# Weights of a two-block transformer kernel in units of 512 columns instead of 1024, with the same bytes of buffer

## The reference

```python
# first block, twice
h = h + _mixer(rmsnorm(h), w_in, w_ret_o, w_sb_o, w_out)   # retention, stick-breaking attention, gates
h = h + (silu(g) * u) @ w_down                             # g, u = rmsnorm(h) @ w_gate_up, FF = 2816
...
# second block, for layer in range(2)
x = x + 0.5 * swiglu(rms_norm(x, g[0]), ffn1_w_in[layer], ffn1_w_out[layer])
x = x + mixed            # layer 0: forgetting and differential attention; layer 1: convolution and banded attention
x = x + memory_cross_attention(rms_norm(x, g[2]), rms_norm(mem, g[3]), ...)
x = x + 0.5 * swiglu(rms_norm(x, g[4]), ffn2_w_in[layer], ffn2_w_out[layer])
```

## Time and profile before

| what | us |
|---|---|
| median of three runs | 1864.65 |
| the profiled execution's own time | 1865.1 |
| its span, first to last instruction | 1862.7 |
| TensorE (PE) busy in the span | 1857.9 |
| VectorE (DVE) busy | 1310.3 |
| ScalarE (ACT) busy | 1119.3 |
| GpSimd (POOL) busy | 369.0 |

### The profile page before, as it was taken

The page is one execution under the profiler, slowest core; times in us unless marked ns, Lnnn a source line. Parts: engine busy times, 40 slices in busy tenths (PEclk is TensorE's granted clock), DMA queues, the critical chain, the costliest instruction groups (busy, mean ns, idle before and its releaser), DMA issues.

```text
span 1862.7 us, 25413 instructions
## 1 busy us (share of the span) xinstructions
PE 1857.9 (100%) x9293; PEld 1623.7 (87%) x9293; DVE 1310.3 (70%) x1949; ACT 1119.3 (60%) x1678; POOL 369.0 (20%) x606
## 2 busy tenths in 40 slices
PE   9999999999999999999999999999999999999999
PEld 8888988888889888888888889888888888899888
DVE  6776776667777776666577886776666578977664
ACT  6776655557766655555468785654555467765553
POOL 2101233111001431122103001531122111102320
PEclk9999999999999999999999999999999999999999
DMA  9767789878578997798765567997798788758984
GB/s 316 236 186 229 222 258 299 260 233 253 166 221 242 292 287 232 219 272 255 238 180 191 174 191 204 281 274 237 225 255 252 227 265 242 216 157 232 255 258 138
DMA packets 289803, 436.43 MB, mean 234 GB/s; under 512 B 25548, under 2 KB 170416, under 8 KB 289424
## 3 DMA queue, kind: packets, MB, share of 16 engines
q1 hardware_dynamic: 260384, 352.41, 61.9%
q0 software_dynamic: 28832, 82.07, 16.3%
q10 hardware_dynamic: 464, 0.34, 0.1%
HBM read 396.43 MB, written 38.29 MB: 233 GB/s over the span
## 4 chain that ended last, share of the span: by engine, by line
PE 99%; DMA 0%; DVE 0%; SPq 0%; ACT 0%; issue 0%; ACTq 0%
PE M L1081 31%; PE M L1083 31%; PE M L1082 31%; PE AUX L1124 1%; PE AUX L1138 0%; PE AUX L1252 0%; DMA RAW<-in_w_in 0%; PE AUX L1244 0%; PE AUX L1242 0%; PE AUX L1279 0%; PE AUX L1167 0%; PE AUX L1295 0%; PE AUX L1323 0%; PE AUX L1296 0%; PE AUX L1297 0%; PE AUX L1324 0%
## 5 line engine op out<-in xcount | busy, mean ns | idle before, releaser
L1647 DVE TENSOR_TENSOR WL<-RAW,WH 128x1024 fp32r<-128x1024 f32 (+1 forms) x669 | 810.8, 1217 | 383.5 <-ACT WH L1358 380.9
L1358 ACT ACTIVATE WH<-RAW 128x1024 fp32r<-128x1024 f32 (+1 forms) x670 | 705.0, 1055 | 518.8 <-PE M L1083 469.7
L1081 PE MATMUL M<-WH,Bh 128*128 128x512 f32 (+1 forms) x1820 | 691.3, 380 | 0.6 <-ACT TMP L1401 0.3
L1082 PE MATMUL M<-WL,Bh 128*128 128x512 f32 (+1 forms) x1820 | 683.1, 375 | 0.0
L1083 PE MATMUL M<-WH,Bl 128*128 128x512 f32 (+1 forms) x1820 | 683.1, 375 | 0.0
L1081 PEld LDWEIGHTS M<-WH,Bh 128*128 128x128 f32 x1820 | 344.2, 189 | 50.6 <-issue 4.2
L1083 PEld LDWEIGHTS M<-WH,Bl 128*128 128x128 f32 x1820 | 344.2, 189 | 47.1
L1082 PEld LDWEIGHTS M<-WL,Bh 128*128 128x128 f32 x1820 | 344.4, 189 | 44.7
L1396 ACT ACTIVATE AS<-M,KEEP 128x256 f32<-128x256 f32 x132 | 55.3, 470 | 80.3 <-PE M L1083 78.7
L1081 PE MATMUL M<-WH,MTh 128*128 128x512 f32 x128 | 51.0, 398 | 0.0
L1082 PE MATMUL M<-WL,MTh 128*128 128x512 f32 x128 | 48.5, 379 | 0.0
(11 more groups left out here) (534 smaller groups left out, 2886.9 us busy)
## 6 DMA issues: line engine op xcount, KB each, us to landing
RAW<-in_ffn_w_in SPq DMA_DIRECT2D x352, 256.0 KB, 4.2
RAW<-in_w_in SPq DMA_DIRECT2D x103, 512.0 KB, 4.8
RAW<-in_w_gate_up SPq DMA_DIRECT2D x176, 256.0 KB, 4.4
RAW<-in_ffn_w_out SPq DMA_DIRECT2D x88, 512.0 KB, 4.6
RAW<-in_w_down SPq DMA_DIRECT2D x44, 512.0 KB, 4.9
RAW<-in_x_w_kv SPq DMA_DIRECT2D x32, 512.0 KB, 4.6
RAW<-in_even_w_in SPq DMA_DIRECT2D x24, 512.0 KB, 4.5
RAW<-in_odd_w_in SPq DMA_DIRECT2D x24, 512.0 KB, 5.4
```

The source lines that it names most:

```text
L1081: e.matmul(out, s.hi, wh, start=s.at0, stop=False)
L1082: e.matmul(out, s.hi, wl, start=False, stop=False)
L1358: e.activation(hi, raw, ACT.Copy).then_inc(k.w_hi, 1)
L1647: e.tensor_tensor(lo, raw, hi.bitcast(F32), ALU.subtract).then_inc(k.w_lo, 1)
```

## The change

It halves the unit and doubles the count of slots and buffers. The bytes of RAW (4 x 1024 = 8 x 512 columns), of WH and of WL (5 x 1024 = 10 x 512) stay. Nothing of `PLACES` and `LATER` changes. The first eight k-blocks were units of 1, 1, 2, 2 and 2 k-blocks and become eight units of one.

```diff
-UC = 1024
-NRAW = 4
-NHL = 5
+UC = 512
+NRAW = 8
+NHL = 10
...
-    first = [(0, 1), (1, 1), (2, 2), (4, 2), (6, 2)]
+    first = [(i, 1) for i in range(8)]
...
-            e.wait_ge(*((k.w_used, s.c.done - 3) if t else (k.tile_done, 1)))
+            e.wait_ge(*((k.w_used, s.c.done - 6) if t else (k.tile_done, 1)))
...
-                        p.add("nfld", p.now + 40.0).done = p.n_unit + 18
+                        p.add("nfld", p.now + 40.0).done = p.n_unit + 36
```

## The result

The changed kernel takes 1874.86 us (median of six runs, 1874.08 to 1875.79) against 1864.62 us for the kernel before (median of six, 1864.44 to 1866.2). The ratio is 1.0052, 95% interval 1.0043 to 1.0062. It is slower by 10.2 us, outside of the range of the prediction. The profiled execution took 1874.99 us, its span is 1872.9 us and the granted clock 1.0.

The account below looks back on a forecast made before the run. TensorE was taken as the bound, busy 1857.9 of 1862.7 us. Opening -0.6 and attention stages +1.4 gave +0.8 on the profiled 1865.1 us, so 1865.9, or 1865.5 against the median; range 1863.2 to 1871.

Parts of the forecast that it names:

- Attention stages: Attention stages: moved convs make some late steps miss their slack, +1.4 us, bounds 0 and 13.
- 21 close points: Attention stages: 21 releases of TensorE with under 0.45 us to spare; each can win 0.5 us or lose 0.6.
- Buffers that come free by halves: Weight buffers: release after each k-block raises the weights' lead from 6.9 to about 10 us, worth nothing where nothing waits.
- VectorE as the bound: Attention stages: added VectorE work overfills its busiest windows, costing 6 to 12 us, 1871 to 1877; chance 0.15.
- 135 and 94: Splits in halves: us of added busy time on ScalarE and VectorE, hidden behind TensorE in feed-forward stages at no cost.
- TensorE's waits and counts: TensorE's matmuls: 667 more waits and 667 more counts, taken as zero; upper bound 47 us, 17 us by the skill.
- The opening: First k-blocks: TensorE's stalls at 14.16 and 17.21 us shrink, a gain of 0.6 us, bounds 0 and 3.3.
- DMA: Weight loads: 934 DMAs become 1337, 575 us of queue issue time, taken as zero; bound 169 us inside queue waits.

Follow-up runs that it names:

- c_pairs: Changed kernel with convs placed two at a time at even k-blocks from unit 10 on; 1864.67 us, ratio 0.9995 to the kernel before.
- l_even_look9: Changed kernel with convs in pairs at even k-blocks and placed for 9 units ahead in place of 10; 1864.65 us, ratio 0.9998 to the kernel before.
- h_dve_halves: Kernel before with only VectorE's 1024-wide subtraction done as two 512-wide instructions; 1866.8 us, ratio 1.0008.
- m_handoff: Kernel before with both engines' splits done as two instructions and VectorE released after ScalarE's first half; 1866.23 us, ratio 1.0008.
- d_dma256: Kernel before with every weight DMA cut to 256 KB; 1865.29 us, ratio 0.9999.
- b_look9: Changed kernel with convs placed for 9 units ahead in place of 10, with ten buffers still; 1869.0 us, ratio 1.0020 to the kernel before.
- k_odd_look9: Changed kernel with convs in pairs at odd k-blocks and placed for 9 units ahead; 1878.0 us, ratio 1.0070 to the kernel before.
- f_pairs_look8: Changed kernel with convs in pairs at even k-blocks and placed for 8 units ahead; 1865.43 us, ratio 1.0007 to the kernel before, single runs 1864.51 to 1871.42.
- o_raw6: Changed kernel with six slots of RAW in place of eight; 1888.73 us, ratio 1.0125 to the kernel before.

## Why the prediction was wrong

**The step that failed is "Attention stages".** It took +1.4 us, one close point in three losing 0.2 us, within bounds of 0 and 13. Measured are 22 places with 11.0 us, 0.5 us each. The stages and the kind of step were the right ones; the size was too small by a factor of eight. It was taken near the low end, with the reason that the queues wait for TensorE for hundreds of us. That reason doesn't hold: a queue that waits for TensorE is not a queue with time to spare if the waiting instruction is a conv and a step that TensorE needs stands behind it. The section priced what a conv *lasts* (0.6 us), not what it *waits* (2.00 and 2.46 us in the two patterns above).

Its list of 21 close points missed many of the places as well. In 17 of the 22 the trace names the step for which TensorE waited. Before the change six of these 17 had ended more than 0.45 us ahead of TensorE's load, up to 1.67 us (L1961 at 1040 us) and with the longest stall's among them (0.51 us); they hold 3.5 us of the loss. Seven places lost more than the 0.6 us which was taken as the most that a point can lose, up to 1.69. So 21 is near 22, and the bound of 13 us held, partly by luck.

The waits of ScalarE's convs for TensorE were 392 before and are 673 after:

```profile
ACT WH L1358 <- PE M L1083: 447.7, 673, 3.0
```

The total of them fell (469.7 us before), while their number rose by 281. Each is a place at which a late step can be caught, if one stands behind it; c_pairs has 546 of them and loses nothing in sum. The step "Buffers that come free by halves", which called the longer lead "worth nothing where nothing waits", has the same fault: it looked at the lead of the weights, and never at who stands behind a conv.

**How the 10.2 us divide.** Taking the convs from the odd k-blocks removes all of it (c_pairs). One buffer in hand removes 5.9 us (1874.86 - 1869.0), by the wait for the buffer; the other 4.3 (1869.0 - 1864.65, to l_even_look9) go by the order alone, and where they were followed, by VectorE's wait for a copy. The split isn't a sum of two independent causes: with the convs at even places the buffer in hand brings nothing (1864.67 without it, 1864.65 with it). It also shortens the lead of the weights by a k-block: in l_even_look9's profiled execution (1866.54 us) the weights ran out twice, at 677 and 681 us, which cost some 2 us. The cause is the odd place, and the buffer wait is how more than half of it acts.

**VectorE as the bound, the rival with 0.15.** Its band, 1871 to 1877 us, holds the result. Its mechanism isn't what happened. It needs seven more k-blocks of work in a window that is full; VectorE's windows fell from 18.71 to 18.26 and from 19.47 to 17.18 us, and c_pairs and l_even_look9 do the same number of instructions at the time of before. That an occupation of 1 or 2 us exists isn't excluded (1.4 us in h_dve_halves, 1.2 in m_handoff, both at the edge of what can be told). That the result lies in its band is luck.

**What was right.** A 512-wide copy took 0.629 us and a subtraction 0.685, as taken. The groups rose by 820.7 - 703.5 = 117 us and 885.4 - 809.4 = 76 us, 135 and 94 being forecast; many halves run back to back and overlap. The feed-forward stages hid them: TensorE is busy for 20.00 us in the first window. The lead of the weights rose from 6.8 to 9.5 us in these stages and from 7.8 to 10.0 over all units after 20 us (medians), a rise from 6.9 to 10 being forecast. Its minimum fell, though, from 3.25 to 0.82 us.

*TensorE's waits and counts*: the starts in the feed-forward stage are still 0.216 us apart.

```profile
1322.24 0.38 PE L1081 MATMUL M<-WH,LA0h 128*128 128x512 f32 x1
1322.46 0.38 PE L1082 MATMUL M<-WL,LA0h 128*128 128x512 f32 x1
...
1323.54 0.38 PE L1081 MATMUL M<-WH,LA0h 128*128 128x512 f32 x1
```

From one k-block to the next it is 1.30 us, with a wait and a count in each now. l_even_look9 has all 667 more counts and stands at 0.9998. The Trainium skill ("TensorE: Matmul & The Clock Gate", The cost: per-tile semaphore tail) has some 26 ns for each increment, by which an estimate is 17 us for them. These runs don't show it, where one matmul in six counts.

*The opening*: both stalls are gone, 14.16 and 17.21 us in the earlier trace rows are now

```profile
14.05 0.38 PE L1081 MATMUL M<-WH,Bh 128*128 128x512 f32 x1
...
16.64 0.38 PE L1081 MATMUL M<-WH,Bh 128*128 128x512 f32 x1
```

The gain by 17 us is 0.57 us, for 0.6 forecast. It isn't the two stalls alone: TensorE also waits 0.8 us for the norm's gains ahead of 5.67 us (L1150) in this execution, and starts a little closer on either side of it make most of that good. *DMA*: nothing that d_dma256 shows. The prediction's 575 us of issues is a slip, 1337 x 0.42 is 562; nothing hangs on it.

**The numbers.** With 21 points under 0.45 us, and an upper bound of 13 us worked out for them, 0.15 for a loss of several us was too little, and 1871 as the upper end left out half of that bound.

**What stays open.** Of the 4.3 us of order, 1.6 lie between 1040 and 1042 us and 1.7 at 1586 us (before's time); the latter was followed through the queues, of the former only VectorE's wait ahead of L1865 was read. In b_look9 the stalls at 228 and 1699 us grew by 0.25 us each, and why is open. k_odd_look9's profiled execution is 1.5 us below its median, so its waits are those of one of its better runs. No version beats the kernel before by more than the measurement tells: the best are c_pairs with 0.9995 (0.9986 to 1.0004) and l_even_look9 with 0.9998. Places in `PLACES` set anew for convs at every k-block weren't tried.

## What to carry to other kernels

Where queues are in order and planned, halving a unit doubles the places at which an instruction asks for a buffer: ask of each what stands behind it, and whether the engine that frees the buffer needs that. The same holds for an instruction that waits for another engine's copy. Let a producer ask for a buffer one unit after it comes free, and keep the places when the grain changes (two halves where one whole stood); here the first was worth 5.9 us and the second all 10.2. Price such a place by the longest wait of the instruction in front (2 to 2.5 us here) less the slack of the step behind it, and not by the time that the instruction takes or by the average idleness of the engines.

## What the runs showed of the hardware

**A stall of 4 us costs more than itself.** In f_pairs_look8's longest run ScalarE waited for a small exchange through DRAM, with convs behind it:

```profile
677.38 0.63 ACT L1450 ACTIVATE FA1h<-HB1t 128x512 fp32r<-128x512 f32 x1 [7.08 <-DMA HB1t<-squares]
```

The lead was used up, TensorE waited 4.02 us, and then the granted clock was about half (windows of 5 us, columns as above):

```profile
675.00:680.00 5.00, 0.98 (x4) 0.52 (x3) 1.90 (x3) 2.56 (x6) 0.00 (x0) 0.79 0.59 143
680.00:685.00 5.00, 5.00 (x14) 3.99 (x13) 4.96 (x11) 4.31 (x10) 2.93 (x5) 0.53 0.73 197
685.00:690.00 5.00, 5.00 (x25) 4.38 (x24) 4.68 (x10) 3.71 (x9) 2.18 (x4) 1.00 1.05 340
```

From 679.39 to 684.67 us matmuls start 0.43 us apart, the level of 1.2 GHz, then 0.216 us again. Twelve starts took 5.28 us in place of 12 x 0.216 = 2.59, so 2.7 us come on top of the 4. That run is 6.0 us above the median of its kernel. It is one execution; in l_even_look9's, where TensorE was idle twice for 0.7 us at the same place, the windows of 5 us show a clock of 1.00 throughout.

**The same exchange is late in the changed kernel too, and is hidden there.** ScalarE's waits for it were 2.8 us in total before and are 30.2 after:

```profile
ACT FA1h L1448 <- DMA HB1t<-squares: 30.2, 10, 8.1
```

d_dma256 has 8.3 us, c_pairs 17.7. The longest is 8.05 us, up to 676.20 us, and seven us later the weights of one unit were ready only 0.8 us before TensorE needed them. So the lead of ten buffers isn't spare. That a fuller stream of weights delays the exchange is a guess which no run here tells apart.

**Slots of RAW.** From eight to six, 13.9 us (o_raw6), by the matmuls' starts some 6.6 us of it by 90 us, 3.8 at 960 to 980 us and 3 near 1600: the distance at which weights are fetched is worth more than the whole loss of the change.
